# RWKV-7 layer of a four-layer kernel: where the gate's low-rank projection stands, and which engines prepare the scan

## The reference, cut to what matters

```python
xs = x[None] + mu[0][:, None, None, :] * dx_prev[None] + mu[1][:, None, None, :] * dx_next[None]
r, k, v = einsum('ibld,ide->ible', xs[:3], w_rkv)
lw = einsum('nblr,nrd->nbld', tanh(einsum('bld,ndr->nblr', xs[3], w1)), w2)      # n: two directions
la = einsum('nblr,nrd->nbld', einsum('bld,ndr->nblr', xs[4], a1), a2)
g  = einsum('blr,rd->bld', sigmoid(einsum('bld,dr->blr', xs[5], g1)), g2)        # g1: 1024 x 160
decay, a = exp(-exp(-softplus(-(w0 + lw)) - 0.5)), sigmoid(a0 + la)
kk = normalised(k * k_k);  kd = k[None] * (1.0 + (a - 1.0) * k_a)
y  = scan over tokens, forwards and backwards, of (r, decay[n], kd[n], v, kk, a[n])
bonus = sum(r * (kd[0] + kd[1]) * r_k) * v
out = ((group_norm(y) + bonus) * g) @ w_o
```

## Time and profile before

| what | value |
|---|---|
| median of three runs | 3012.98 us (3008.86 to 3021.1) |
| the profiled execution | 3013.64 us, of which its span is 3011.8 us |
| last v product to first kk product | 588 to 596 us of the span |
| first kk product to first G of direction 0 | 595.8 to 641.9 us |
| first G of direction 0 to first G of direction 1 | 641.9 to 680.7 us |
| rest of the scan | 680.7 to 957 us |

### The profile page before, as it was taken

How to read it: one execution, slowest core, us unless ns; L and a number is a source line. 1 busy time by engine, 2 the same in 40 slices (tenths; PEclk the granted TensorE clock), 3 DMA queues, 4 the chain that set the end, 5 groups by cost and what they waited for, 6 DMA issues and landing times.

```text
span 3011.8 us, 58574 instructions
## 1 busy us (share of the span) xinstructions
PE 2630.5 (87%) x25328; PEld 2406.7 (80%) x25328; DVE 2023.9 (67%) x3067; ACT 1547.4 (51%) x2519; POOL 406.8 (14%) x261
## 2 busy tenths in 40 slices
PE   7868997968878699999999999998657798888898
PEld 7637996847776589999999999997554698877898
DVE  4574436764334489999999999997454576355673
ACT  3334433462112267777777777775433354354452
POOL 2002430021100100000000000000050143121242
PEclk9858998957797799999999999999786799989999
DMA  5102442300001279999999999996230144332342
GB/s 214 60 1 105 180 176 93 116 1 4 18 4 59 87 269 359 336 348 352 340 363 335 345 358 336 361 343 236 74 113 7 63 168 172 138 130 80 126 177 111
DMA packets 83209, 538.94 MB, mean 179 GB/s; under 512 B 9488, under 2 KB 9488, under 8 KB 38912
## 3 DMA queue, kind: packets, MB, share of 16 engines
q1 hardware_dynamic: 82368, 531.08, 47.9%
q0 software_dynamic: 576, 4.06, 0.4%
HBM read 534.05 MB, written 1.05 MB: 178 GB/s over the span
## 4 chain that ended last, share of the span: by engine, by line
PE 73%; DVE 17%; ACT 7%; issue 2%; POOL 1%; DMA 0%; DVEq 0%; SPq 0%; ACTq 0%; POOLq 0%
PE ps L564 19%; PE ps L565 18%; PE ps L566 18%; PE ps L1330 2%; ACT sh L509 2%; DVE sl L519 2%; DVE arena_conv L2731 2%; PE ps L570 2%; PE ps L1841 1%; DVE xl L560 1%; PE ps L612 1%; PE ps L1324 1%; PE ps L1286 1%; DVE arena_conv L2733 1%; ACT xh L555 1%
## 5 line engine op out<-in xcount | busy, mean ns | idle before, releaser
L2061 DVE TENSOR_TENSOR sl<-ring,sh 128x1024 fp32r<-128x1024 f32 x613 | 735.0, 1219 | 29.6 <-ACT sh L2019 18.0
L564 PE MATMUL ps<-xh,sh 128*128 128x256 f32 (+1 forms) x1856 | 557.6, 300 | 101.8 <-DVE xl L560 66.1
L2019 ACT ACTIVATE sh<-ring 128x1024 fp32r<-128x1024 f32 x613 | 630.5, 1053 | 2.0 <-DVE xl L1901 1.9
L564 PE MATMUL ps<-sh,xh 128*128 128x256 f32 (+2 forms) x2012 | 595.5, 296 | 13.6 <-POOL sl L526 6.0
L565 PE MATMUL ps<-sl,xh 128*128 128x256 f32 (+2 forms) x2012 | 575.9, 286 | 0.0
L566 PE MATMUL ps<-sh,xl 128*128 128x256 f32 (+2 forms) x2012 | 575.1, 286 | 0.0
L565 PE MATMUL ps<-xl,sh 128*128 128x256 f32 (+1 forms) x1856 | 547.4, 295 | 0.0
L566 PE MATMUL ps<-xh,sl 128*128 128x256 f32 (+1 forms) x1856 | 544.5, 293 | 0.0
L526 POOL TENSOR_TENSOR sl<-ring,sh 128x1024 fp32r<-128x1024 f32 (+4 forms) x102 | 249.7, 2449 | 1861.4 <-PE ps L570 1037.7
L564 PEld LDWEIGHTS ps<-xh,sh 128*128 128x128 f32 x1856 | 369.2, 199 | 123.9 <-DVE xl L560 78.2
L509 ACT ACTIVATE sh<-ring 128x1024 fp32r<-128x1024 f32 (+1 forms) x341 | 338.2, 1021 | 169.9 <-PE ps L566 161.5
(11 more groups left out here) (531 smaller groups left out, 4248.0 us busy)
## 6 DMA issues: line engine op xcount, KB each, us to landing
ring<-ws_d SPq DMA_DIRECT2D x229, 1024.0 KB, 7.1
ring<-ws_d SPq DMA_DIRECT2D x80, 1536.0 KB, 6.5
ring<-ws_d SPq DMA_DIRECT2D x226, 512.0 KB, 6.8
ring<-ws_d SPq DMA_DIRECT2D x24, 1408.0 KB, 6.0
ring<-ws_d SPq DMA_DIRECT2D x4, 1256.0 KB, 5.5
ring<-ws_d SPq DMA_DIRECT2D x2, 1088.0 KB, 4.9
scan_t<-scn_d POOLq DMA_DIRECT2D x1, 1824.0 KB, 8.1
ring<-ws_d SPq DMA_DIRECT2D x1, 1248.0 KB, 5.8
```

The costliest lines, as they stand in the source:

```text
L564: e.matmul(out, ah, bh, start=start, stop=False)
L2019: e.activation(out, raw(u)[:, a:z], ACT.Copy).then_inc(*af.on("high", u, i))
L2061: e.tensor_tensor(l, raw(u)[:, a:z], f32(h), SUB).then_inc(s_fd if i < 2 else s_fp, 1)
```

## The change

The gate's projection leaves the project stage. Three new generators, `late_pe`, `late_dve` and `late_act`, are drawn ahead of each of direction 0's six preparation steps. PE's queue becomes: w2 and a2 of the first half, the eight products of lg's 128-column tile, the eight of its 32-column tile, w2 and a2 of the second half. DVE's mixes of input 5 stand in three portions: blocks 0 to 2 ahead of the first half's accumulation, 3 to 5 behind it, 6 and 7 ahead of the operand products. PE no longer interleaves lg's two tiles. The KK multiplications follow one another. All mixes of input 4 stand ahead of the wait for the root of the norms.

PE's scan starts at ACT's mark "project" (HW and HA written), ACT's at its constants alone; DVE still waits for the marks of all engines. POOL's part of the scan goes away but for one DMA: KK x a and key factor x K are made by DVE in the second step of each half, behind the mixes of that step; the identities are two ACT copies a chunk, one step after ACT's eviction of N; the bonus sum is made by DVE, its scaling by an ACT Identity. In the bonus, `quad` of block k - 1 is made behind the second step of block k on PE (it was the fourth step of its own block), and DVE evicts it in that same round.

The second tile of lg is packed in 256 columns, where it was padded to 1,024. Direction 0's work tiles begin behind it, at BW + 256; its PC moves to `scan_t`.

```diff
-    t += tiles_of("lg", g("rw_g1", 0), 8, [(0, 128), (128, 32)], 128)
+    t += tiles_of("lg", g("rw_g1", 0), 8, [(0, 128), (128, 32)])
...
             for n, i in enumerate(tiles[name]):
+                b, free = psum.take((name, n))
+                wv, cw, ready = raw_tile(i)
+                w.wait_ge(*free, ready)
+                for k in range(8):
+                    w.wait_ge(dv["mixed", m, k])
+                    e.matmul(PS[0:cw, b, 0:T0], wv[:, k, 0:cw], xs[:, k, :], start=k == 0, stop=k == 7).then_inc(*pe.on("lora", m, n, k))
                 pe.mark(name, n)
                 block_ends(i)
+                yield
...
-            lora_pe(w, e, 5, "lg")
             pe.mark("project")
+
+        def late_pe(w, e):
+            yield
+            yield
+            yield from lora_pe(w, e, 5, "lg")
+            yield
+            yield
...
+        def late_dve(w, e):
+            for ks in ((0, 1, 2), (3, 4, 5), (6, 7), (), (), ()):
+                for k in ks:
+                    mix_dve(w, e, 5, k, XF[1][:, k, :], pe["lora", 3, 0, k])
+                yield
...
+        def late_act(w, e):
+            for _ in range(3):
+                yield
+            for n, r in enumerate((128, 32)):
                 w.wait_ge(pe["lg", n])
-                e.activation((HG, HG2[0:32])[n], PS[0:r, psum["lg", n], 0:T0], ACT.Sigmoid).then_inc(*ac.on())
+                e.activation((HG, HG2[0:32])[n], PS[0:r, psum["lg", n], 0:T0], ACT.Sigmoid).then_inc(*ac.on("lg", n))
                 psum.gone["lg", n] = [ac.now()]
+                yield
+            yield
...
             for _ in range(PREPARE):
+                next(late)
                 next(runs[0])
...
-            w.wait_ge(*bar("project"), IN_SCN)          # scan_pe
+            w.wait_ge(ac["project"], IN_SCN)
...
-            w.wait_ge(*bar("project"))                  # scan_act
+            w.wait_ge(IN_SCN, IN_PAR)
...
+                def identity(ci):
+                    if ci < NC:
+                        w.wait_ge(*([pe["N", n, ci - 1]] if ci else [dv["prepared", n, 1]]))
+                        for v in (d.X, d.Y):
+                            e.activation(v, sn("id2")[:, None, :].broadcast_to([128, 8, 64]), ACT.Copy).then_inc(*ac.on())
+                        ac.mark("identity", n, ci)
...
                     e.tensor_tensor(t1, A, t1, SUB).then_inc(*dv.on("shifted", n, hf))
                     yield
+                    w.wait_ge(ac["sigmoid", "a2", n, hf, 3])
+                    e.tensor_tensor(B, kk, t2, MUL).then_inc(*dv.on())
+                    w.wait_ge(ac["key factors", n, hf])
+                    e.tensor_tensor(K, K, Kr[:, d0, :], MUL).then_inc(*dv.on("keys", n, hf))
                     yield
...
                 for k in range(8):
                     va = VV[:, k, :]
                     yield
+                    w.wait_ge(ac["out a", 1, k])
+                    e.tensor_tensor(va, va, va1, ADD).then_inc(*dv.on("out b", k))
+                    quad(k - 1)
+                    yield
+                    yield
+                    w.wait_ge(ac["key of out", k])
+                    e.tensor_tensor(va, va, Kr[:, k, :], MUL).then_inc(*dv.on())
...
-            w.wait_ge(*bar("project"), IN_SCN)          # scan_pool
...
+            w.wait_ge(*bar("project"), dv["quad", 7])
+            e.dma_start(ow, ow_d).then_inc(s_in["ow"], 16)
```

More of the change, by code:

```diff
@@ L1097, in project_dve @@
                 split_low(w, e, i)
-                lora(3, n)
-            for k in range(3):
-                lora(4, k)
+                mix_dve(w, e, 3, n, XF[1][:, n, :])
+            for k in range(8):
+                mix_dve(w, e, 4, k, XF[0][:, k, :], pe["after", "rkv1"])
             w.wait_ge(ac["kk root"])
@@ L1163, in sn @@
             return scn[:, sc[name][0]:sc[name][0] + sc[name][1]]
-        ka_rest = cut(scan_t, 8 * 8 * T0 + ns, 8)
+        ka_rest, ka_rest2 = (cut(scan_t, 8 * 8 * T0 + ns + 8 * i, 8) for i in range(2))
         ring_flat = ring[:, :, :].rearrange("p a b -> p (a b)")
@@ L1393, in bonus @@
                     yield
[L1394 to L1397, removed]
+                    if k:
+                        colsum_pe(w, e, ("quad", k - 1), "blk", VV[:, k - 1:k, :], 1, T0, dv["quad", k - 1])
+                    for _ in range(3):
+                        yield
+                yield
+                colsum_pe(w, e, ("quad", 7), "blk", VV[:, 7:8, :], 1, T0, dv["quad", 7])
                 for _ in range(BEFORE_GATES):
@@ L1468, in steps @@
                     if ci < NC - 1:
+                        identity(ci + 1)
                         yield
@@ L1497, in scan_dve @@
             w.wait_ge(*bar("project"), IN_SCN, IN_PAR)
-            e.tensor_scalar(ka_rest, par("k_a"), -1.0, 1.0, MUL, ADD).then_inc(*dv.on("k_a rest"))
+            for i, v in enumerate((ka_rest, ka_rest2)):
+                e.tensor_scalar(v, par("k_a"), -1.0 - i, 1.0 + i, MUL, ADD).then_inc(*dv.on())
+            dv.mark("k_a rest")
             def steps(n):
@@ L1543, in steps @@
                         yield
-                    w.wait_ge(po["identity", *u], dv.now(), pe["Ut", *u])
+                    w.wait_ge(ac["identity", *u], dv.now(), pe["Ut", *u])
                     b = psum["Ut", *u]
@@ L1589, in steps, with quad @@
                     yield
+            def quad(k):
+                if k >= 0:
+                    w.wait_ge(pe["quad", k])
+                    e.tensor_tensor(VV[:, k, :], PS[:, psum["quad", k], 0:T0], Vr[:, k, :], MUL).then_inc(*dv.on("bonus", k))
+                    psum.gone["quad", k] = [dv.now()]
             def bonus():
@@ L1600, in bonus @@
                     yield
[L1601 to L1605, removed]
+                yield
+                quad(7)
+                for _ in range(BEFORE_GATES):
                     yield
@@ L1610, in bonus @@
                     e.scalar_tensor_tensor(out=VV[:, k, :], in0=VV[:, k, :], scalar=par("lnx_b")[:, k:k + 1], in1=gate[:, k, :], op0=ADD, op1=MUL).then_inc(*dv.on())
-            streams(steps, bonus)
+            streams(steps, bonus, late_dve(w, e))
             dv.mark("scan")
         def scan_pool(w, e):
-            w.wait_ge(*bar("project"), IN_SCN)
[L1618 to L1649, removed]
-                w.wait_ge(dv["quad", 7])
-                e.dma_start(ow, ow_d).then_inc(s_in["ow"], 16)
-            streams(steps, bonus)
+            w.wait_ge(*bar("project"), dv["quad", 7])
+            e.dma_start(ow, ow_d).then_inc(s_in["ow"], 16)
             po.mark("scan")
```

58 lines of the change are left out of this document (24 added, 34 removed).

## The result

The changed kernel took 2996.49 us at the median of four runs (2991.35 to 3000.42), the kernel before 3016.95 us at the median of four (3008.86 to 3021.1). The ratio is 0.9934, with a 95% interval of 0.9905 to 0.9964: 20 us faster, 0.66 per cent. The forecast was 3007 with a range of 2996 to 3016, and 0.84 for a change within half a per cent. The time is inside the range by half a microsecond, at the corner where the clock stays up and all waits go, and the likeliest class was not the one that came. As a difference the forecast was 6.1 us, a third of what was measured.

A forecast was written before the change was run, and what follows sets the result against it. It took one thin thread to bound 588 to 642 us, and PE to be busy 96.25 of 109.40 us in the scan. Terms -2.5 (to first G), +0.4 (direction 1), -4.0 (rest of scan) gave 3012.98 - 6.1 = 3007, range 2996 to 3016.

The forecast's parts named there:

- the clock stays up: Rival, up to first G: -8.7 in place of -2.5, about 3001, or 2996 with all waits gone; chance 0.14.
- Steps 1, 2 and 4: Before first G: input 4's moved mixes cost nothing; kk stays PE-bound, ending 599.64; DVE finishes the first half at 619.6.
- The full-clock bound: Up to first G, everything at 0.475 us a product: G at 633.2, -8.7.
- Steps 3, 5 and 6: Before first G, half clock: first-half w2/a2 599.64 to 606.9, lg's second tile to 622.5, second-half w2/a2 to 629.8, G 640.5.
- -2.5: Gain taken up to first G, between -1.4 at half clock and -8.7 at full clock.
- The products on DVE: Preparation before first G: POOL's two products held DVE up by 4.3 us; on DVE they take 1.20 each.
- Direction 1's preparation: Beside chunk 0, from G to G: DVE's new products hold up X1 by some 0.4; +0.4, bounds 0 and 1.6.
- `quad`: Bonus rounds of the scan: PE's waits of 1.8 and 6.6 mostly go, bound -8.4, less than half remains: -3.5.
- The identities on ACT: Scan chunks: two ACT copies, 1.2 us a chunk, hidden behind N's eviction: 0; bound +9.6.
- The rival on the other side: Scan: a T waits 1.2 us behind two identity copies on ACT; 3020.5 with all eight; chance 0.11.
- The waits only move: Rival, scan: PE waits one step later for what it no longer waits for at quad's eviction; 3011; chance 0.17.
- the clock of the chunks: Sign of being wrong: the scan's granted clock moves from 0.78 by more than 0.05.

The follow-up runs named there:

- experiment 2: Kernel before with only the engine moves, quad evicted in its own round and the new packing; old project stage and scan start: 3000.98 us, ratio 0.995.
- experiment 6: Kernel before with only quad's making and eviction moved, to the second step of the next block: 3010.45 us, ratio 0.9969.
- experiment 8: Changed kernel with the gate's mixes early, its products behind all of direction 0's preparation and its sigmoids behind the exponentials: 2990.28 us, ratio to before 0.9897.
- experiment 3: Changed kernel with the two products of each half back on POOL: 2999.54 us in one run.

## Why the prediction was right or wrong

**Steps 1, 2 and 4 held.** Five mixes of input 4 cost nothing; kk was followed at once by w2 (600.02, with kk's own start 0.45 later than before). DVE's list was to be done with the first half at 619.6: its last product ran from 618.46 to 619.74, in an execution that began 0.45 later.

**The full-clock bound was right.** With everything at full clock the prediction had lg's second tile done at 618.7, w2 and a2 at 622.5 and G at 633.2; measured were 619.2, 623.1 and 633.5.

**Steps 3, 5 and 6: the clock.** w2 and a2 of the first half were at half clock, as said. The step that failed in size is the choice of -2.5 between -1.4 and -8.7, made because "w2 and a2 ran at half clock wherever they stood". In all three profiles of the changed kernel the second half's ran in 3.93 us, at full clock, since lg stood in front of them. And before was no evidence to the contrary. The very trace that was read has two rows against "wherever they stood": the stretch ahead of the 0.50, in which the first of these products ran, and four w2 products of direction 1 in 2.10 us, 0.53 each:

```profile
612.00:616.00 4.00, 4.00 (x13) 0.72 0.00 0
...
658.11 2.10 PE L1268 MATMUL ps<-arena,scan_t 64*128 64x272 f32 x8
```

All 16 products of direction 0 stand behind lg there, and the third profile of before has them in this row of PE's timeline:

```profile
612.05 7.57 PE L1268 MATMUL ps<-arena,scan_t 64*128 64x272 f32 x32 [0.96 <-ACT arena L1147]
```

That is 0.47 us a product, full clock. The second profile of before and those of experiments 2 and 6, with lg in the same place, have 7.57 us too. Only the first profile of before took 13.14 us for them, and its row at 616 to 620 with 0.50 is the one that I read as a rule. It was what one execution happened to do. Without lg in front (experiment 8) they take 0.90 us each. The thread lost 8.8 us in the first pair and 7.4 on average of three, so this term was mis-sized by 5.

The rule of the Trainium skill ("TensorE: Matmul & The Clock Gate", section "What's actually happening"), full clock while PE is kept busy, would have given the -8.7. The trace does not agree with it: PE was busy 4.00 of 4.00 us at 0.50 from 604 to 608 in the changed kernel. The number came out through lg.

**The products on DVE.** The reading that POOL's products held DVE up is shown by experiment 3, at 2.70 us for 0.50, and costs 2.4 of the 3.2 us that the thread is longer there.

**Direction 1's preparation:** +0.4 expected, -0.9 on average, of which most is one profile at a higher clock (35.3). The two others are within 0.4 of before's. A term of this size is not tested by that.

**`quad`:** -3.5 was expected, on the ground that "less than half remains" of 8.4 us of waits. The move alone gave 8 us at the median (ratio 0.9969), the whole bound, and no less than 4 by the interval; by the scans of all profiles it is 5 to 8. The mechanism was right and the discount too large. In the first pair of profiles the scan's length hid it, because one kernel's scan differs by 6 to 9 us from one execution to the next.

**The identities on ACT:** hidden, as said. The rival on the other side is out by the traces, in which no T stood behind a copy; the ratios of 0.9936 and 0.9934 agree with that but could not exclude a few microseconds. The contention of POOL's copies, for which I took -0.5, is below what was measured.

**The rivals.** "The clock stays up" happened where it was placed, for the thread. "The waits only move" looked true after the first pair and is refuted by experiment 6 as an account of the time; of PE's idle time a part did only move, 4 of 8 us on average. I had each as the exception to the forecast; the gains of the thread (7.4) and of `quad` (about 8) added up instead, to 15 of the 20 us. The sign that I had set for being wrong, the clock of the chunks off its 0.78 by more than 0.05, came true in the second profile of the changed kernel (0.85); but it differs as much between executions of one kernel, so it tells little of the change. That the time lies in the range is in part luck: its lower end was the one rival, the clock that stays up, taken together with all waits gone, and the measured time is 0.5 us above it. And 0.84 for no measurable change was too sure for a sum that hung on two discounts.

**Open.** Five of the 20 us are not explained. Some 3 us of the difference lie behind the first gather and 1 in the output stage, where no instruction was changed. The ten profiles of kernels with the gate's second tile in the new packing took 1955.7 to 1959.4 us behind the first gather, the four with the old packing (before three times, and experiment 6) 1959.5 to 1961.5; experiment 2, with the old order and the new packing, has 1957.6. Whether the shifted weight stream, the clock or chance does this was not tried. Nor is it shown why the clock fell during w2 and a2 in the first profile of before, where all others of that order ran them at full.

## What to carry to other kernels

When queues are interleaved by hand and PSUM banks are taken in turn, look for a bank that is evicted one round late: here eight such evictions gave six waits of PE, 6.6 us in all. Evict it in the round in which it is made. Look for the engine that idles right ahead of the thread (here DVE's 6 us and PE's 10 us) and put the independent work there, not in front of the thread's own products. Before sizing a change in a stretch whose granted clock differs from one execution to the next (0.78 to 0.87 here, for one kernel), take several profiles: one pair can hide or invent 6 to 9 us in 276. And compare stretches between marks of the work, not windows of equal length.

## What the runs showed of the hardware that was not expected

The same program, with the same order on each engine, had a granted clock of 0.78 over one execution of the scan and 0.87 over another, and the scan took 276.1 and 266.9 us; a third execution had 0.81 and took 276.2. The products of 64 rows for w2 and a2 took 0.89 to 0.95 us each directly behind the 16-row products of kk, though PE had not been idle, and stayed at that for all 16 of them in experiment 8; directly behind lg's products of 128 rows they took 0.49 or less in every profile but one, the first of before, where 16 of them took 13.14 us. Four accumulations on DVE took 4.73 us beside POOL's products and 2.57 without.
